# A third exponentials buffer, grouped sample products and six banks for the K/V slabs in the attention stream of a hybrid decoder step

## The chip, the cores and the metric

The kernel runs on one core of one Trainium2 chip. The metric is the device time of one execution in microseconds. Everything is float32; the large products are split into a high and a low part (three products each).

## The reference, cut to what matters

Four half-layers over 1024 prompt tokens and 32 sample tokens (8 sequences of 4). First an mLSTM layer and its MLP, then K and V are projected once, then one sliding-window attention layer with its MLP, then a final norm.

```
kv = rmsnorm(x, kv_norm) @ w_kv                    # shared K/V: 4 heads of 64
q  = rmsnorm(x, norm_mix[l]) @ w_q[j]              # 16 query heads of 64
s  = einsum(q, k) * 64**-0.5 + bias                # prompt: blocks of 128 queries on 256 keys
s  = where(valid, s, -inf)                         # sample: 32 rows on 128 cached + 4 new keys
m  = maximum(max(s), sink)
e  = exp(s - m)
p  = e / (sum(e) + exp(sink - m))
x  = x + (p @ v) @ w_attn_out[j]
x  = x + relu(rmsnorm(x, norm_ffn[l]) @ w_up)**2 @ w_down
```

What is in question is the middle of this: the K/V projection, and the attention with its q and output projections. Outputs are the two hidden states, the mLSTM states and the key and value windows.

## The kernel before

All activations are held transposed, features on partitions and the 1056 tokens along the free dimension, in three blocks of 352 tokens. Each engine has one hand-written instruction stream, in order; they meet at counting semaphores. Weights come in slabs of 128x1024 numbers, two buffers: SP loads a slab, ACT rounds it (`w_hi`, L682), DVE makes the remainder (`w_lo`, L1031), and PE multiplies.

The attention part has 20 slabs in the order `ATT`: kv2 and kv3 (values), kv0 and kv1 (keys), q0 to q5, four output slabs, q6, q7, four output slabs. A slab is eight chunks; a chunk is nine matmuls of 352 columns (L1864 to L1866: three token blocks by three products). Block g of a slab's output has one of four PSUM banks (`att_block`, L345: g % 4), and before PE starts block g it waits until block g-4 has been taken by DVE (L1424 for K/V, L1426 for q, L1443 for output slabs). The blocks of K/V need the token scale `rstd`: its sums are two matmuls inside slab kv2 (L1623, L1624, L1627), after which DVE (L1049) and ACT (L715) finish it.

The values are needed with tokens on partitions. After chunk 18 PE transposes all of them at once (sixteen transposes, L1962) into banks 4 to 7 and DVE copies them to `v_tok` (L1528). The last pieces follow after chunk 34 (L1973, L1540 to L1542). SP waits for the first copies (`kvt_taken`, L610) before it loads the sample's cache into `act_a` and `act_b`, and the loads of later slabs are behind that in its queue.

From chunk 42 on the attention runs as 64 units (8 head pairs by 8 blocks of 128 queries). Unit u's steps are spread over the engines' loops. In iteration u of its loop, each engine does the following:

- PE: `scores(u+1)` into banks 4 and 5, the dense chunks of `att_window(u)` (one chunk in each of iterations 0 to 29, then 0 to 6), `transposes(u-1)` into bank 6, `values(u-2)` into bank 7, and a step of the sample. 
- DVE: `maxima(u)` (L1460: adds the bias and writes the logits to `prob`, with the maxima), `probabilities(u-1)` (L1467, L1470), `outputs(u-3)` (L1476), then the dense evacuations and splits of the window, then a step of the sample.
- ACT: `exps(u)` (L881), dense splits, `copy_t(u-1)` (L890, the transposed probabilities out of PSUM), and at u % 8 == 2 the rounding of a finished head pair (`o_high`, L897).
- POOL: the sink column of unit u (L1005), and at u % 8 == 3 a remainder (`o_low`, L997).

`prob` has two buffers (u % 2). So `maxima(u)` and the sink column of u wait for the transposes of u-2:

```
if u >= 2:
    dve.wait_ge(t_ready, u - 1)
```

PE's `scores(u)` waits for `maxima(u-1)` (`mx_ready`), since banks 4 and 5 are single.

The sample (all 8 sequences, per half of the heads) runs as steps 0 to 8 beside units 23 to 31 and again beside 55 to 63. Step 6 multiplies probabilities and values: in each of two halves, for each of four sequences, a product over 128 cached keys and one over the 32 new ones, both into the same 32 partitions of the bank, one after the other (L1947, L1948). Its probabilities are first copied from the bank to `sp_t` and `sp_new` (L1506, L1507). The scores of steps 2 and 3 (L1932, L1933) have the same order.

Of the kernel before, what the change touches and what calls it, by code (L numbers as in the profile page):

```python
# [20 lines left out]
P = 128  # L21
# [6 lines left out]
TB = 3  # L28
# [154 lines left out]
def build(nc, io):  # L183
    with ExitStack() as ctx:
# [114 lines left out]
        k_past, v_past = (x[:, 0:DEC_B * P].rearrange("p (b n) -> p b n", b=DEC_B) for x in (act_a, act_b))  # L299
        prob = sb("prob", [P, 2, 2, 2 * WIN + 2], where=phase)  # L300
        prob_t = sb("prob_t", [P, 2, 4, P], where=phase)
        stat = sb("stat", [P, 2, 6], where=phase)
        s_stat = sb("s_stat", [P, 6], where=phase)
# [3 lines left out]
        s_prob = sb("s_prob", [P, 2, SKEY + 1], where=phase)  # L307
        sp_t = sb("sp_t", [P, 2, P], where=phase)
        sp_new = sb("sp_new", [SAMP, 2, P], where=phase)
        phase.close()  # L310
# [34 lines left out]
        def att_block(g):  # L345
            return acc[:, g % 4, 0:TN]

# [120 lines left out]
        def _(sp):  # L468
# [138 lines left out]
            def load_cache(gp):  # L607
                heads = slice(2 * gp, 2 * gp + 2)
                if gp == 0:
                    sp.wait_ge(kvt_taken, 1)  # L610
                for dst, name, last_read in ((k_past, "cache_k", 2), (v_past, "cache_v", 6)):
                    if gp > 0:
                        sp.wait_ge(sk_ready, last_read)
                    sp.dma_start(dst, io[name][:, :, heads, :].rearrange("b s g d -> s b (g d)")
                                 ).then_inc(samp_in, 16)

            def store_kv():
                sp.wait_ge(kvt_taken, 2)
# [55 lines left out]
        def _(act):  # L674
# [201 lines left out]
            def exps(u):  # L876
                r, lo = u % 2, WIN if u % NCH == 0 else 0
# [74 lines left out]
        def _(pool):  # L952
# [48 lines left out]
            for u in range(UNITS):  # L1001
                n = u // NCH
                if u >= 2:
                    pool.wait_ge(t_ready, u - 1)
                nc.gpsimd.tensor_copy(prob[:, u % 2, :, 2 * WIN], by_head[:, n // 4, n % 4]).then_inc(sink_col, 1)  # L1005
# [12 lines left out]
        def _(dve):  # L1018
# [431 lines left out]
            def maxima(u):  # L1450

                n, b = divmod(u, NCH)
                r, lo, head = u % 2, WIN if b == 0 else 0, 8 * (n // 4) + n % 4
                if u >= 2:
                    dve.wait_ge(t_ready, u - 1)
                if b == 0:
# [7 lines left out]
            def probabilities(u):  # L1464
                r, lo = u % 2, WIN if u % NCH == 0 else 0
# [12 lines left out]
            def sample(gp, step):  # L1478
# [25 lines left out]
                if step == 6:  # L1504
                    dve.wait_ge(sk_ready, 7 * gp + 5)
                    V.tensor_copy(sp_t[:], bank[:, 0:256].rearrange("p (a n) -> p a n", a=2))  # L1506
                    V.tensor_copy(sp_new[:], bank[0:SAMP, 256:512].rearrange("p (a n) -> p a n", a=2)).then_inc(sk_taken, 1)  # L1507
                if step == 7:
# [15 lines left out]
            dve.wait_ge(rstd_ready, 3)  # L1524
            att_dense(range(4, 22))
            dve.wait_ge(kvt_ready, 1)
            for q in range(4):
                x = V.tensor_copy(v_tok[:, 2 * q:2 * q + 2], acc[:, 4 + q].rearrange("p (t n) -> p t n", t=2))  # L1528
            x.then_inc(kvt_taken, 1)
            dve.wait_ge(bias_in, 16)  # L1530
# [7 lines left out]
            att_dense(range(32, 36))  # L1538
            dve.wait_ge(kvt_ready, 2)
            V.tensor_copy(v_tok[0:SAMP, NCH], acc[0:SAMP, 4, 0:256])  # L1540
            V.tensor_copy(k_new[:, 0], acc[:, 5, 0:256])
            V.tensor_copy(k_new[0:SAMP, 1], acc[0:SAMP, 5, 256:512]).then_inc(kvt_taken, 1)  # L1542
            att_dense(range(36, 42))
# [30 lines left out]
        def _(pe):  # L1574
# [261 lines left out]
            def att_dense(chunks):  # L1836

                for i in chunks:
# [17 lines left out]
                    for b in range(TB):  # L1856
                        g = BLK0 + TB * (AFIRST[p] + n) + b
                        if kk == 0 and g >= BLK0 + 4:
                            pe.wait_ge(blk_taken, g - 3)
                        elif kk == 0:  # L1860
                            pe.wait_ge(out_taken, O_KV - (1 if g < BLK0 + 3 else 0))
                        if (kind, j, k, b) == ("q", 5, 0, 0):
# [11 lines left out]
            def scores(u):  # L1874
                n, b = divmod(u, NCH)
                gp, lo = n // 4, WIN if b == 0 else 0
                if b == 0:
                    pe.wait_ge(q_ready, n + 1)
                if u == 0:
                    pe.wait_ge(kvt_taken, 2)  # L1880
                else:
                    pe.wait_ge(mx_ready, u)
# [6 lines left out]
            def transposes(u):  # L1889
                r = u % 2  # L1890
                pe.wait_ge(pr_ready, u + 1)
                if u >= 1:
                    pe.wait_ge(tc_ready, u)
                for e in range(2):
# [18 lines left out]
            def sample(gp, step):  # L1913
# [12 lines left out]
                if step in (2, 3):  # L1926
# [3 lines left out]
                    for b in range(4):  # L1930
                        rows = slice(SAMP * b, SAMP * b + SAMP)
                        T.matmul(bank[rows, 0:WIN], q_m[:, 4 * half + b], kp_t[:, 4 * half + b], start=True, stop=True)  # L1932
                        x = T.matmul(bank[rows, WIN:SKEY], q_m[:, 4 * half + b], k_t[:, gp, SEQ:], start=True, stop=True)  # L1933
                    x.then_inc(sk_ready, 1)
# [6 lines left out]
                if step == 6:  # L1941
                    pe.wait_ge(sk_taken, 6 * gp + 5)
                    for half in range(2):
                        for b in range(4):
                            rows = slice(SAMP * b, SAMP * b + SAMP)
                            out = bank[rows, P * half:P * half + P]
                            T.matmul(out, sp_t[:, half, rows], v_past[:, 4 * half + b], start=True, stop=False)  # L1947
                            x = T.matmul(out, sp_new[:, half, rows], v_tok[0:SAMP, NCH, P * gp:P * gp + P], start=False, stop=True)  # L1948
# [9 lines left out]
            pe.wait_ge(ssum_taken, 6)  # L1958
            for t in range(NCH):
                for g, v in enumerate((act_a, act_b)):  # L1960
                    at = 256 * (t % 2) + P * g
                    x = T.transpose(acc[:, 4 + t // 2, at:at + P], v[:, cols(t)], ident[:])  # L1962
            x.then_inc(kvt_ready, 1)
            att_dense(range(19, 35))
            pe.wait_ge(blk_taken, BLK0 + 4 * TB)
            pe.wait_ge(kvt_taken, 1)
            for g, v in enumerate((act_a, act_b)):
                T.transpose(acc[0:SAMP, 4, P * g:P * g + P], v[:, cols(NCH)], ident[:])
            for i, t in enumerate((NCH - 1, NCH)):
                n = size(t)  # L1970
                for g in range(2):
                    at = 256 * i + P * g
                    x = T.transpose(acc[0:n, 5, at:at + P], k_t[:, g, cols(t)], ident[:])  # L1973
            x.then_inc(kvt_ready, 1)
# [98 lines left out]
```

## Time and profile before

| | |
|---|---|
| three runs | 2568.69, 2572.0, 2572.22 us, median 2572.0 |
| profiled execution, its own time | 2562.05 us |
| its span | 2560.2 us, mean granted TensorE clock 0.984 |
| PE busy | 2453.5 us (96%) |
| PE weight loads | 2331.1 us (91%) |
| DVE, ACT, POOL busy | 1155.2, 656.1, 159.5 us |
| attention part, first K/V matmul to last output chunk | about 1364 to 1782 us of the span |

The profile lists PE twice: weight loads (PEld) and matmuls (PE). A matmul's end is modelled and overlaps its follower, so a row of PE that reads "busy" may still hold a stop; the idle time printed beside a weight load is the nearer measure of how long PE stood. Numbers in square brackets are the idle time of that engine just before the row, with what ended it.

### The profile page before, as it was taken

The numbers are of one execution on the slowest core, as the hardware profiler recorded it, in microseconds if no ns is written. First come the engines' busy times: TensorE is split into PE (matmuls) and PEld (weight loads), VectorE is DVE, ScalarE is ACT, GpSimd is POOL, SyncE is SP. The second block draws the span as 40 slices with busy tenths as digits, with TensorE's granted clock in tenths as the row PEclk, the third lists the DMA queues.
The fourth block names the chain that finished last, engine by engine and source line by source line (L and its number), as shares of the span: only waits on it lengthen the run. The fifth ranks groups of instructions, "written<-read, shape, count | busy, mean of one in ns | idle before, by whom it ended". The sixth has DMA issues, their size and how long they took to land.

```text
span 2560.2 us, 36896 instructions
## 1 busy us (share of the span) xinstructions
PE 2453.5 (96%) x15530; PEld 2331.1 (91%) x15530; DVE 1155.2 (45%) x2023; ACT 656.1 (26%) x1080; POOL 159.5 (6%) x208
## 2 busy tenths in 40 slices
PE   6999999988999999999998989989999999999998
PEld 6889898877999999999998866868999999999997
DVE  6545555566434333333345554465433333333333
ACT  3232222233212111111222443254212112112113
POOL 3000000002000000000002011013000000000002
PEclk8999999999999999999999998999999999999999
DMA  3111121110111111111111311101111111111111
GB/s 108 44 46 52 46 64 37 43 35 25 50 50 50 42 42 50 42 44 47 44 47 53 91 28 46 34 9 41 42 45 47 42 50 42 42 50 50 42 50 68
DMA packets 177416, 120.53 MB, mean 47 GB/s; under 512 B 23624, under 2 KB 173045, under 8 KB 177221
## 3 DMA queue, kind: packets, MB, share of 16 engines
q1 hardware_dynamic: 177108, 118.10, 15.7%
q8 instruction: 132, 2.16, 0.4%
q14 instruction: 32, 0.25, 0.0%
q10 hardware_dynamic: 144, 0.02, 0.0%
HBM read 110.94 MB, written 12.33 MB: 48 GB/s over the span
## 4 chain that ended last, share of the span: by engine, by line
PE 89%; DVE 7%; issue 1%; ACT 1%; POOL 1%; DMA 1%; SPq 0%; DVEq 0%; ACTq 0%
PE acc L1589 58%; PE acc L1669 5%; PE acc L1671 4%; PE acc L1670 4%; PE acc L1864 3%; PE acc L1866 3%; PE acc L1865 3%; DVE prob L1460 2%; PE acc L1885 2%; DVE rstd L1049 1%; PE acc L1897 1%; PE acc L1725 1%; DVE w_lo L1031 1%; PE acc L1692 1%; PE acc L1710 1%
## 5 line engine op out<-in xcount | busy, mean ns | idle before, releaser
L1589 PE MATMUL acc<-x_hi,w_hi 128*128 128x352 f32 x1560 | 340.0, 326 | 14.8 <-DVE x_lo L1037 6.2
L682 ACT ACTIVATE w_hi<-w_raw 128x1024 fp32r<-128x1024 f32 x180 | 189.2, 1051 | 618.4 <-PE acc L1589 527.6
L1062 DVE TENSOR_TENSOR x_res<-x_res,acc 128x1056 f32<-128x1056 f32 x128 | 160.4, 1253 | 413.6 <-PE acc L1589 413.6
L1589 PE MATMUL acc<-x_hi,w_lo 128*128 128x352 f32 x1560 | 336.6, 323 | 0.0
L1589 PE MATMUL acc<-x_lo,w_hi 128*128 128x352 f32 x1560 | 336.4, 324 | 0.0
L1589 PE MATMUL acc<-h_hi,w_hi 128*128 128x352 f32 x1536 | 332.1, 324 | 0.0
L1589 PE MATMUL acc<-h_hi,w_lo 128*128 128x352 f32 x1536 | 331.1, 323 | 0.0
L1589 PE MATMUL acc<-h_lo,w_hi 128*128 128x352 f32 x1536 | 330.6, 323 | 0.0
L1589 PEld LDWEIGHTS acc<-x_hi,w_hi 128*128 128x128 f32 x1560 | 266.0, 189 | 18.1 <-issue 13.0
L1589 PEld LDWEIGHTS acc<-x_hi,w_lo 128*128 128x128 f32 x1560 | 268.0, 188 | 0.0
L1589 PEld LDWEIGHTS acc<-x_lo,w_hi 128*128 128x128 f32 x1560 | 265.6, 188 | 0.0
L1589 PEld LDWEIGHTS acc<-h_hi,w_lo 128*128 128x128 f32 x1536 | 263.6, 188 | 0.0
L1589 PEld LDWEIGHTS acc<-h_hi,w_hi 128*128 128x128 f32 x1536 | 261.7, 189 | 0.0
L1589 PEld LDWEIGHTS acc<-h_lo,w_hi 128*128 128x128 f32 x1536 | 260.9, 188 | 0.0
L1031 DVE TENSOR_TENSOR w_lo<-w_raw,w_hi 128x1024 fp32r<-128x1024 f32 x180 | 236.8, 1316 | 21.5 <-ACT w_hi L682 21.4
L1055 DVE TENSOR_TENSOR act_a<-acc,rstd 128x1056 f32<-128x1056 f32 x64 | 80.5, 1257 | 331.9 <-PE acc L1589 329.6
L1669 PE MATMUL acc<-x_hi,w_hi 128*128 128x352 f32 x576 | 197.4, 343 | 2.6 <-DVE pair L1177 2.6
L845 ACT ACTIVATE act_b<-act_a 128x1056 f32<-128x1056 f32 x64 | 69.6, 1087 | 501.8 <-DVE act_a L1055 501.8
L1671 PE MATMUL acc<-x_hi,w_lo 128*128 128x352 f32 x576 | 188.4, 327 | 0.0
L1670 PE MATMUL acc<-x_lo,w_hi 128*128 128x352 f32 x576 | 188.0, 326 | 0.0
L1669 PEld LDWEIGHTS acc<-x_hi,w_hi 128*128 128x128 f32 x576 | 110.5, 192 | 11.1 <-issue 4.6
L1385 DVE TENSOR_TENSOR h_lo<-act_a,h_hi 128x1056 fp32r<-128x1056 f32 x64 | 80.6, 1259 | 73.8 <-ACT h_hi L847 73.8
(265 smaller groups left out, 3112.1 us busy)
## 6 DMA issues: line engine op xcount, KB each, us to landing
w_raw<-in_w_up SPq DMA_DIRECT2D x64, 512.0 KB
w_raw<-in_w_down SPq DMA_DIRECT2D x64, 512.0 KB
w_raw<-in_w_mlstm_in SPq DMA_DIRECT2D x24, 512.0 KB
x_in<-in_x_prompt SPq DMA_DIRECT2D x8, 512.0 KB, 4.0
w_raw<-in_w_mlstm_out SPq DMA_DIRECT2D x8, 512.0 KB
w_raw<-in_w_q SPq DMA_DIRECT2D x16, 256.0 KB
w_raw<-in_w_attn_out SPq DMA_DIRECT2D x16, 256.0 KB
out_y_prompt<-y_out SPq DMA_DIRECT2D x8, 512.0 KB, 2.6
```

The costliest lines, as they stand in the source:

```text
L682: nc.scalar.activation(w_hi[:, s.parity], w_raw[:, s.parity], ACT.Copy).then_inc(hi_split, 1)
L1031: V.tensor_tensor(w_lo[:, s.parity], w_raw[:, s.parity], w_hi[:, s.parity].bitcast(F32), ALU.subtract).then_inc(lo_split, 1)
L1055: x = V.tensor_tensor(blocks(dst), group(o), blocks(rstd[:]), ALU.mult)
L1062: V.tensor_tensor(blocks(x_res[:, k]), blocks(x_res[:, k]), group(o), ALU.add).then_inc(out_taken, 1)
L1385: V.tensor_tensor(h_lo[:, half, c], act_a[:], h_hi[:, half, c].bitcast(F32), ALU.subtract).then_inc(hl_ready, 1)
L1589: last = T.matmul(out[:, b], w[:, k, m], x[:, TN * b:TN * b + TN], start=(k == 0 and i == 0), stop=(k == k_chunks - 1 and i == 2))
L1669: T.matmul(block_of(g), hi, mh[:, span(b)], start=(kk == 0), stop=False)
L1670: T.matmul(block_of(g), hi, ml[:, span(b)], start=False, stop=False)
L1671: x = T.matmul(block_of(g), lo, mh[:, span(b)], start=False, stop=(kk == n_k - 1))
L1864: T.matmul(att_block(g), hi, mh[:, span(b)], start=(kk == 0), stop=False)
L1865: T.matmul(att_block(g), hi, ml[:, span(b)], start=False, stop=False)
L1866: x = T.matmul(att_block(g), lo, mh[:, span(b)], start=False, stop=(kk == n_k - 1))
```

## The change

Three edits. `prob` and `stat` get three buffers; `maxima`, the sink column, `exps`, `probabilities` and `transposes` use u % 3, and the waits of DVE and POOL are for the transposes of u-3. To make room, `sp_t` and `sp_new` move into `act_a`, where the cached keys have been read by then; the second load of the keys waits for step 6.

In sample steps 2, 3 and 6 the four products on the cache are issued first, then the four on the new tokens.

The blocks of the four K/V slabs rotate over six banks, (g - BLK0) % 6, and wait for block g-6; later blocks stay with four. Banks 4 and 5 are thus in use, so the value transposes use banks 6 and 7 alone, in two halves: after chunk 18 and after chunk 20. `kvt_taken` counts three steps; the cache load waits for the second, and the wait for the third moves from `scores(0)` to `transposes(0)`.

```
-        prob = sb("prob", [P, 2, 2, 2 * WIN + 2], where=phase)
+        sp_t = act_a[:, 0:2 * P].rearrange("p (a n) -> p a n", a=2)
+        sp_new = act_a[0:SAMP, 2 * P:4 * P].rearrange("p (a n) -> p a n", a=2)
+        prob = sb("prob", [P, 3, 2, 2 * WIN + 2], where=phase)
...
         def att_block(g):
-            return acc[:, g % 4, 0:TN]
+            bank = g % 4 if g >= BLK0 + 4 * TB else (g - BLK0) % 6
+            return acc[:, bank, 0:TN]
...
             def load_cache(gp):
-                    sp.wait_ge(kvt_taken, 1)
-                for dst, name, last_read in ((k_past, "cache_k", 2), (v_past, "cache_v", 6)):
+                    sp.wait_ge(kvt_taken, 2)
+                for dst, name, last_read in ((k_past, "cache_k", 6), (v_past, "cache_v", 6)):
...
-                if u >= 2:
-                    pool.wait_ge(t_ready, u - 1)
+                if u >= 3:
+                    pool.wait_ge(t_ready, u - 2)
...
             def maxima(u):
-                r, lo, head = u % 2, WIN if b == 0 else 0, 8 * (n // 4) + n % 4
-                if u >= 2:
-                    dve.wait_ge(t_ready, u - 1)
+                r, lo, head = u % 3, WIN if b == 0 else 0, 8 * (n // 4) + n % 4
+                if u >= 3:
+                    dve.wait_ge(t_ready, u - 2)
...
-            att_dense(range(4, 22))
-            dve.wait_ge(kvt_ready, 1)
-            for q in range(4):
-                x = V.tensor_copy(v_tok[:, 2 * q:2 * q + 2], acc[:, 4 + q].rearrange(...))
-            x.then_inc(kvt_taken, 1)
+            att_dense(range(4, 20))
+            for i in range(2):
+                dve.wait_ge(kvt_ready, i + 1)
+                for q in range(2):
+                    x = V.tensor_copy(v_tok[:, 4 * i + 2 * q:4 * i + 2 * q + 2], acc[:, 6 + q].rearrange(...))
+                x.then_inc(kvt_taken, 1)
+                att_dense(range(20 + i, 21 + i))
...
                         g = BLK0 + TB * (AFIRST[p] + n) + b
-                        if kk == 0 and g >= BLK0 + 4:
+                        if kk == 0 and g >= BLK0 + 5 * TB:
                             pe.wait_ge(blk_taken, g - 3)
+                        elif kk == 0 and g >= BLK0 + 2 * TB:
+                            pe.wait_ge(blk_taken, g - 5)
...
             def transposes(u):
-                r = u % 2
+                r = u % 3
                 pe.wait_ge(pr_ready, u + 1)
-                if u >= 1:
-                    pe.wait_ge(tc_ready, u)
+                pe.wait_ge(*((kvt_taken, 3) if u == 0 else (tc_ready, u)))
...
                 if step == 6:
                     for half in range(2):
                         for b in range(4):
                             rows = slice(SAMP * b, SAMP * b + SAMP)
+                            T.matmul(bank[rows, P * half:P * half + P], sp_t[:, half, rows], v_past[:, 4 * half + b],
+                                     start=True, stop=False)
+                        for b in range(4):
+                            rows = slice(SAMP * b, SAMP * b + SAMP)
                             out = bank[rows, P * half:P * half + P]
-                            T.matmul(out, sp_t[:, half, rows], v_past[:, 4 * half + b], start=True, stop=False)
                             x = T.matmul(out, sp_new[:, half, rows], v_tok[0:SAMP, NCH, P * gp:P * gp + P], start=False, stop=True)
...
             att_dense(range(19))
-            for t in range(NCH):
-                for g, v in enumerate((act_a, act_b)):
-                    x = T.transpose(acc[:, 4 + t // 2, at:at + P], v[:, cols(t)], ident[:])
-            x.then_inc(kvt_ready, 1)
-            att_dense(range(19, 35))
+            for i in range(2):
+                if i == 1:
+                    pe.wait_ge(kvt_taken, 1)
+                for t in range(4 * i, 4 * i + 4):
+                    for g, v in enumerate((act_a, act_b)):
+                        x = T.transpose(acc[:, 6 + t % 4 // 2, at:at + P], v[:, cols(t)], ident[:])
+                x.then_inc(kvt_ready, 1)
+                att_dense(range(19 + 2 * i, 21 + 2 * i))
+            att_dense(range(23, 35))
```

## Rows read from the trace of the kernel before

**Rows 1.** The page: busy times of the engines, shares of the span, instructions.
```profile
PE 2453.5 (96%) x15530; PEld 2331.1 (91%) x15530; DVE 1155.2 (45%) x2023; ACT 656.1 (26%) x1080; POOL 159.5 (6%) x208
```

**Rows 2.** Timeline (start, length in us) of PE, early in slab kv3.
```profile
1377.54 0.32 PE L1865 MATMUL acc<-x_lo,w_hi 128*128 128x352 f32 x1
1377.70 0.32 PE L1866 MATMUL acc<-x_hi,w_lo 128*128 128x352 f32 x1
1384.78 0.66 PE L1864 MATMUL acc<-x_hi,w_hi 128*128 128x352 f32 x1 [6.75 <-DVE act_a L1424]
```

**Rows 3.** Timeline of DVE and ACT, same slabs.
```profile
1376.29 6.75 DVE L1049 RECIPROCAL rstd<-rstd 128x1056 f32<-128x1056 f32 x1
1384.19 1.38 DVE L1424 TENSOR_TENSOR act_a<-acc,rstd 128x352 f32<-128x352 f32 x3 [1.15 <-ACT rstd L715]
1385.50 1.21 DVE L1031 TENSOR_TENSOR w_lo<-w_raw,w_hi 128x1024 fp32r<-128x1024 f32 x1
1398.13 1.06 ACT L682 ACTIVATE w_hi<-w_raw 128x1024 fp32r<-128x1024 f32 x1 [13.02 <-PE acc L1866]
```

**Rows 4.** Waits from 1437 to 1745 us: us in total, times, longest.
```profile
PEld acc L1885 <- DVE stat L1460: 34.2, 49, 2.1
...
PEld acc L1885 <- issue: 6.4, 13, 1.2
```

**Rows 5.** Timeline of a usual unit, DVE and weight loads.
```profile
1470.42 0.48 DVE L1460 CUSTOM_DVE_ANT_0 prob<-acc,bias,sinks 128x256 f32<-128x256 f32 x1 [1.95 <-PE acc L1897]
1471.37 0.30 PEld L1885 LDWEIGHTS acc<-k_t,q_t 64*128 64x128 f32 x4 [0.64 <-DVE stat L1460]
1471.82 0.28 DVE L1476 COPY q_t<-acc 128x128 f32<-128x128 f32 x1
...
1474.92 0.30 PEld L1885 LDWEIGHTS acc<-k_t,q_t 64*128 64x128 f32 x4 [0.64 <-DVE stat L1460]
```

**Rows 6.** Timeline: score loads behind something other than the transposes.
```profile
1439.05 0.30 PEld L1885 LDWEIGHTS acc<-k_t,q_t 64*128 64x128 f32 x4 [1.08 <-DVE stat L1460]
...
1459.50 0.48 DVE L1460 CUSTOM_DVE_ANT_0 prob<-acc,bias,sinks 128x256 f32<-128x256 f32 x1
1460.45 0.30 PEld L1885 LDWEIGHTS acc<-k_t,q_t 64*128 64x128 f32 x4 [1.16 <-DVE stat L1460]
...
1699.96 0.30 PEld L1885 LDWEIGHTS acc<-k_t,q_t 64*128 64x128 f32 x4 [1.16 <-DVE stat L1460]
```

**Rows 7.** Timeline: a score load whose data was long there.
```profile
1528.12 0.30 PEld L1885 LDWEIGHTS acc<-k_t,q_t 64*128 64x128 f32 x4 [0.17 <-issue]
```

**Rows 8.** Window: us; PE, PEld, DVE, ACT, POOL busy; clock. Waits, 1701 to 1717.3.
```profile
1704.00:1708.00 4.00, 4.00 (x35) 2.49 (x32) 3.68 (x18) 2.75 (x9) 0.19 (x1) 1.00 0.01 2
...
PEld acc L1885 <- DVE stat L1460: 1.3, 4, 0.6
```

**Rows 9.** Weight loads: step 6 of both halves, step 2.
```profile
1551.10 0.14 PEld L1947 LDWEIGHTS acc<-act_b,sp_t 128*32 128x32 f32 x2 [1.00 <-DVE sp_new L1507]
1558.73 0.51 PEld L1885 LDWEIGHTS acc<-k_t,q_t 64*128 64x128 f32 x4 [0.38 <-issue]
...
1718.77 0.14 PEld L1947 LDWEIGHTS acc<-act_b,sp_t 128*32 128x32 f32 x2 [0.17 <-issue]
1724.10 0.30 PEld L1885 LDWEIGHTS acc<-k_t,q_t 64*128 64x128 f32 x4 [0.20 <-issue]
...
1535.08 0.18 PEld L1932 LDWEIGHTS acc<-kp_t,q_m 128*32 128x32 f32 x8 [0.17 <-issue]
1535.55 0.30 PEld L1885 LDWEIGHTS acc<-k_t,q_t 64*128 64x128 f32 x4
```

**Rows 10.** A window as in rows 8, and step 7's loads in both halves.
```profile
1556.00:1560.00 4.00, 4.00 (x15) 1.43 (x16) 0.43 (x1) 0.00 (x0) 0.00 (x0) 0.50 0.00 0
...
1562.00 0.29 PEld L1953 LDWEIGHTS acc<-ident,s_prob 128*128 128x128 f32 x2 [0.33 <-issue]
...
1725.91 0.20 PEld L1953 LDWEIGHTS acc<-ident,s_prob 128*128 128x128 f32 x2 [0.17 <-issue]
```

More of the change, by code:

```diff
@@ L299, in build @@
         k_past, v_past = (x[:, 0:DEC_B * P].rearrange("p (b n) -> p b n", b=DEC_B) for x in (act_a, act_b))
-        prob = sb("prob", [P, 2, 2, 2 * WIN + 2], where=phase)
+        sp_t = act_a[:, 0:2 * P].rearrange("p (a n) -> p a n", a=2)
+        sp_new = act_a[0:SAMP, 2 * P:4 * P].rearrange("p (a n) -> p a n", a=2)
+        prob = sb("prob", [P, 3, 2, 2 * WIN + 2], where=phase)
         prob_t = sb("prob_t", [P, 2, 4, P], where=phase)
-        stat = sb("stat", [P, 2, 6], where=phase)
+        stat = sb("stat", [P, 3, 6], where=phase)
         s_stat = sb("s_stat", [P, 6], where=phase)
@@ L307, in build @@
         s_prob = sb("s_prob", [P, 2, SKEY + 1], where=phase)
-        sp_t = sb("sp_t", [P, 2, P], where=phase)
-        sp_new = sb("sp_new", [SAMP, 2, P], where=phase)
         phase.close()
@@ L617, in store_kv @@
             def store_kv():
-                sp.wait_ge(kvt_taken, 2)
+                sp.wait_ge(kvt_taken, 3)
                 for new, name in ((k_new[:, 0, :], "k_prompt"), (v_tok[:, NCH - 1, :], "v_prompt")):
@@ L876, in exps @@
             def exps(u):
-                r, lo = u % 2, WIN if u % NCH == 0 else 0
+                r, lo = u % 3, WIN if u % NCH == 0 else 0
                 act.wait_ge(mx_ready, u + 1)
@@ L1002, in _ @@
                 n = u // NCH
-                if u >= 2:
-                    pool.wait_ge(t_ready, u - 1)
-                nc.gpsimd.tensor_copy(prob[:, u % 2, :, 2 * WIN], by_head[:, n // 4, n % 4]).then_inc(sink_col, 1)
+                if u >= 3:
+                    pool.wait_ge(t_ready, u - 2)
+                nc.gpsimd.tensor_copy(prob[:, u % 3, :, 2 * WIN], by_head[:, n // 4, n % 4]).then_inc(sink_col, 1)
                 if u >= 11 and u % 8 == 3:
@@ L1464, in probabilities @@
             def probabilities(u):
-                r, lo = u % 2, WIN if u % NCH == 0 else 0
+                r, lo = u % 3, WIN if u % NCH == 0 else 0
                 dve.wait_ge(ex_ready, u + 1)
@@ L1505, in sample @@
                     dve.wait_ge(sk_ready, 7 * gp + 5)
-                    V.tensor_copy(sp_t[:], bank[:, 0:256].rearrange("p (a n) -> p a n", a=2))
-                    V.tensor_copy(sp_new[:], bank[0:SAMP, 256:512].rearrange("p (a n) -> p a n", a=2)).then_inc(sk_taken, 1)
+                    V.tensor_copy(sp_t, bank[:, 0:256].rearrange("p (a n) -> p a n", a=2))
+                    V.tensor_copy(sp_new, bank[0:SAMP, 256:512].rearrange("p (a n) -> p a n", a=2)).then_inc(sk_taken, 1)
                 if step == 7:
@@ L1524, in _ @@
             dve.wait_ge(rstd_ready, 3)
-            att_dense(range(4, 22))
-            dve.wait_ge(kvt_ready, 1)
-            for q in range(4):
-                x = V.tensor_copy(v_tok[:, 2 * q:2 * q + 2], acc[:, 4 + q].rearrange("p (t n) -> p t n", t=2))
-            x.then_inc(kvt_taken, 1)
+            att_dense(range(4, 20))
+            for i in range(2):
+                dve.wait_ge(kvt_ready, i + 1)
+                for q in range(2):
+                    x = V.tensor_copy(v_tok[:, 4 * i + 2 * q:4 * i + 2 * q + 2], acc[:, 6 + q].rearrange("p (t n) -> p t n", t=2))
+                x.then_inc(kvt_taken, 1)
+                att_dense(range(20 + i, 21 + i))
             dve.wait_ge(bias_in, 16)
@@ L1538, in _ @@
             att_dense(range(32, 36))
[L1539 to L1542, printed above, removed]
+            dve.wait_ge(kvt_ready, 3)
+            V.tensor_copy(v_tok[0:SAMP, NCH], acc[0:SAMP, 6, 0:256])
+            V.tensor_copy(k_new[:, 0], acc[:, 7, 0:256])
+            V.tensor_copy(k_new[0:SAMP, 1], acc[0:SAMP, 7, 256:512]).then_inc(kvt_taken, 1)
             att_dense(range(36, 42))
@@ L1857, in att_dense @@
                         g = BLK0 + TB * (AFIRST[p] + n) + b
-                        if kk == 0 and g >= BLK0 + 4:
+                        if kk == 0 and g >= BLK0 + 5 * TB:
                             pe.wait_ge(blk_taken, g - 3)
+                        elif kk == 0 and g >= BLK0 + 2 * TB:
+                            pe.wait_ge(blk_taken, g - 5)
                         elif kk == 0:
-                            pe.wait_ge(out_taken, O_KV - (1 if g < BLK0 + 3 else 0))
+                            pe.wait_ge(out_taken, O_KV - (1 if g < BLK0 + TB else 0))
                         if (kind, j, k, b) == ("q", 5, 0, 0):
@@ L1878, in scores @@
                     pe.wait_ge(q_ready, n + 1)
-                if u == 0:
-                    pe.wait_ge(kvt_taken, 2)
-                else:
+                if u > 0:
                     pe.wait_ge(mx_ready, u)
@@ L1945, in sample @@
                             rows = slice(SAMP * b, SAMP * b + SAMP)
+                            T.matmul(bank[rows, P * half:P * half + P], sp_t[:, half, rows], v_past[:, 4 * half + b],
+                                     start=True, stop=False)
+                        for b in range(4):
+                            rows = slice(SAMP * b, SAMP * b + SAMP)
                             out = bank[rows, P * half:P * half + P]
-                            T.matmul(out, sp_t[:, half, rows], v_past[:, 4 * half + b], start=True, stop=False)
                             x = T.matmul(out, sp_new[:, half, rows], v_tok[0:SAMP, NCH, P * gp:P * gp + P], start=False, stop=True)
@@ L1958, in _ @@
             pe.wait_ge(ssum_taken, 6)
-            for t in range(NCH):
-                for g, v in enumerate((act_a, act_b)):
-                    at = 256 * (t % 2) + P * g
-                    x = T.transpose(acc[:, 4 + t // 2, at:at + P], v[:, cols(t)], ident[:])
-            x.then_inc(kvt_ready, 1)
-            att_dense(range(19, 35))
+            for i in range(2):
[3 more added lines that the diff above has]
+                    for g, v in enumerate((act_a, act_b)):
+                        at = 256 * (t % 2) + P * g
+                        x = T.transpose(acc[:, 6 + t % 4 // 2, at:at + P], v[:, cols(t)], ident[:])
+                x.then_inc(kvt_ready, 1)
+                att_dense(range(19 + 2 * i, 21 + 2 * i))
+            att_dense(range(23, 35))
             pe.wait_ge(blk_taken, BLK0 + 4 * TB)
-            pe.wait_ge(kvt_taken, 1)
+            pe.wait_ge(kvt_taken, 2)
             for g, v in enumerate((act_a, act_b)):
-                T.transpose(acc[0:SAMP, 4, P * g:P * g + P], v[:, cols(NCH)], ident[:])
+                T.transpose(acc[0:SAMP, 6, P * g:P * g + P], v[:, cols(NCH)], ident[:])
             for i, t in enumerate((NCH - 1, NCH)):
@@ L1972, in _ @@
                     at = 256 * i + P * g
-                    x = T.transpose(acc[0:n, 5, at:at + P], k_t[:, g, cols(t)], ident[:])
+                    x = T.transpose(acc[0:n, 7, at:at + P], k_t[:, g, cols(t)], ident[:])
             x.then_inc(kvt_ready, 1)
```

## The prediction

> **What bounds the kernel now.** I read the page's busy times first: PE is busy 96% of the span, every other engine under half [rows 1]. So time is gained only where PE stands, or where its clock is low. The windows over the attention part (1364 to 1782 us) show both, at three places, and the change has an edit for each. The timelines and the table of waits then say what ends each stop.
>
> The first is at the start of slab kv3: PE has done three of its 72 matmuls and stands 6.75 us until DVE's first evacuation [rows 2], which waits for the reciprocal of 6.75 us and the root behind it [rows 3]. The first matmul afterwards lasts 0.66 us where its kind took 0.32 just before [rows 2]: the clock had fallen.
>
> The second is once in nearly every unit. The reader is to follow one round: `maxima` starts at 1470.42, released by the transposes, and `scores` starts 0.95 us later, released by `maxima`, having stood 0.64 us; the next round is 3.55 us on and the same [rows 5]. The waits sum to 34.2 us in 49 times [rows 4].
>
> The third is the sample's step 6: 16 pairs of loads from 1551.10 to 1558.73 in the first half of the heads, 1718.77 to 1724.10 in the second [rows 9], with the clock at 0.50 in the first [rows 10].
>
> **K/V slabs on six banks.** kv3's three blocks no longer wait for kv2's evacuation. From 1377.70 the remaining 69 matmuls go on at the pitch of 0.16 us [rows 2]: 1377.70 + 69 x 0.16 = 1388.7 for the last start; with 0.32 for it and 0.05 for the signal ACT's rounding of the next slab starts at 1389.1, where it started at 1398.13 [rows 3]. That is 9.0 us: 6.75 of stop, the rest the clock. What must be there at 1388.7: the remainder of slab kv0, done at 1385.50 + 1.21 = 1386.7, and kv2's first block taken, by about 1384.7 [rows 3]. So the 2.0 us of slack cover both; if the root came 3 us later, 1 us would come back. The value transposes stay sixteen; that they are in two halves adds a PE wait for two copies, covered by the two chunks between, and DVE work in the same amount. The cache load sits on SP's queue until the second copies, about three us of PE's work later than now, with the q slabs' loads queued behind it; their slabs are needed some twenty chunks on. I take these at nothing. Without a covering row I bound them by 2 us lost. Ends for the edit: 6.7 and 9.0; taken 9.0.
>
> **Third buffer.** `maxima(u)` then waits for the transposes of u-3, done a round earlier, and for `scores(u)`, which PE issues at the head of the round before. In a round of 3.55 us [rows 5] it can be done some 1.7 us in, and PE asks for it at the end. What does not vanish: a score load whose data was long there stands 0.17 us too [rows 7].
>
> The sum over all score loads: 34.2 us in 49 waits, and of the 6.4 us in 13 under "issue" six (4.7 us) are the same stop by position, seven are the 0.2 to 0.4 us ones [rows 4]. So 38.9 us in 55. From this comes off:
> - Ten that end with another thing. The first is the stream's start, 1.08 us; where DVE evacuates a q slab before the next `maxima`, as at 1460.45, `maxima` starts at 1459.50 without waiting for PE [rows 6], and the third buffer can't bring it earlier. Four such of 1.16 us (the last at 1699.96), further 1.22, 1.27, 0.86, 0.37, and 2.06 us behind the sample's step 8. Together 11.5 us.
> - Five from 1701 to 1717 (1.3 us in four [rows 8], and one of 0.7): there are no dense chunks there, and DVE is busy 3.68 of 4 us [rows 8], so DVE is the bound. 2.0 us, taken as kept.
>
> 38.9 - 11.5 - 2.0 = 25.4 us in 40 waits, of which 40 x 0.17 = 6.8 stay: 18.6 us gained. What is late next in the usual round: nothing on PE; DVE's `outputs(u-3)` will be what DVE waits for, with the values one round old. The ends: 0, if another wait takes the place; 38.9 - 55 x 0.17 = 29.6, if every one goes. I take 18.6.
>
> **Grouped products.** At full clock step 6 takes 5.33 us for 16 pairs, 0.333 a pair, of which most is a pause at each change between 128-row and 32-row products [rows 9]. Step 2 has sixteen loads of 32 columns without such a change in 0.47 us [rows 9], so eight take 0.24. The new order has four groups of eight with one pause each. By the rows a group is 0.24 + 0.2 = 0.44; I take 0.5, as eight products of 128 columns have less to overlap with than step 2's mix. 5.33 - 4 x 0.5 = 3.3 us a half, 6.7 in both. Ends: 0, if the pause comes with every product, and 7.1. Steps 2 and 3 have no pause to lose: nothing.
>
> The pause is the trace's (rows 9: 0.333 us a pair against 0.06 for a pair of step 2). The Trainium skill ("TensorEngine Tiling (Array Packing)", Key Properties) says that changing the tiling mode, not just the tile, drains the engine; by that rule the order by shape is what counts, and the trace agrees. Against the change speaks another sentence of it ("TensorE: Matmul & The Clock Gate", Part 3, The mechanism): loads overlap running matmuls only when the row group differs, and here all four products of a group use the same rows. By that rule a group would be 8 x (27 + 53) ns + 0.2 = 0.84 us, an estimate from the page's column times, and the edit would give 2.0 us a half instead of 3.3: 2.7 us less in all. Step 2 has the same row group throughout and its 0.47 us speak for the shorter time.
>
> **Clock.** The first half's step 6 took 7.63 us against 5.33 in the second: 2.3 us at the low clock [rows 9]. From the load of `scores` behind it to step 7's it took 1562.00 - 1558.73 = 3.27 us, in the second half 1725.91 - 1724.10 = 1.81 [rows 9, 10]: 1.5 us. The clock fell while PE worked at a third of its density; with 2 us of products in place of 5.3 I expect no fall there: 3.8 us. The second half had the same sparse 5.3 us with no fall, so this is a matter of phase, and may not repeat: ends 0 and 5, and a fall elsewhere could cost 3.
>
> **Sum.** 9.0 + 18.6 + 6.7 + 3.8 = 38.1 us. The profiled execution's own time is 2562.05 us (span 2560.2): 2524 us. The three runs had 2568.69, 2572.0 and 2572.22, 10 us above it at the median; I carry the difference over: 2572.0 - 38.1 = 2534 us.
>
> **Rivals.** (a) The units find another stop. For it: DVE's stream is in order, with `outputs`, the splits of 1.21 us and evacuations of 1.4 us between two `maxima`, and ACT has its exponentials behind `copy_t`, which waits for PE. Against it: each is needed a round later than it is issued. If two thirds of the 18.6 are lost: 2534 + 12 = 2546 us. (b) The products keep their pauses, by each change of column group, and the clock falls as before: 2534 + 6.7 + 3.8 = 2544 or 2545 us. Against it the 0.47 us of step 2. (c) The other side: the deeper rotation makes DVE wait in every unit for the values before it gets to `maxima`. Now `outputs` never waits in the stretch shown (it starts right after the probabilities [rows 5]); then DVE is a round ahead and it will. Were this for the values of the same round, `maxima` would begin after them and the 0.28 us copy. PE's value loads end 0.64 us before 1471.37, at 1470.73; with 0.3 for the last product, 0.28 for the copy and 0.95 for `maxima`, `scores` starts at 1472.2 or 0.85 us later than before [rows 5]. In 62 units 53 us, against 19.5 from the other edits: 2572 + 33 = 2605 us. It decides if the awaited values lie less than 1.7 us before `maxima`'s due time; the code takes those of u-3, a whole round older. (d) The six banks only move the stop: kv0 waits for its weights or the copies hold up PE, and 7 us of the 9 come back: 2541 us.
>
> **Chances.** Forecast 0.72, (a) 0.14, (b) 0.06, (c) 0.04, (d) 0.04. About 0.2% (5 us) is what a measurement of this kernel can tell from no change. Faster than that holds in all but (c) and in combinations of (a), (b) and (d): 0.92; within it 0.03, slower 0.05. Range: the high end of the terms, with some of the ten or five waits gone too, gives 2523; (a) together with part of (b) gives 2556.
>
> **What would show it.** In the profile after: no idle time before L1864 near 1378, and ACT's rounding of the next slab at about 1389; `maxima` no longer released by the transposes but by L1885, and before most score loads 0.17 instead of 0.64 us; 1.16 us kept before the score load after each q slab's last chunk; waits of L1885 for L1460 down from 34 to about 12 us; step 6 in 2 us; no window at 0.50 after it. Wrong would be: `transposes` (L1897) waiting for L1470 in units with a dense chunk, or DVE's copy of the outputs ahead of each `maxima` with PE standing behind it; loads of step 6 still 0.17 us apart; kv0 late for `w_lo`.

## The result, and the profile after

The changed kernel takes 2527.45 us at the median of four runs (2526.38 to 2529.18), beside 2570.35 us for the kernel before (2564.59 to 2572.22, four runs). The ratio is 0.9841, 95% interval 0.982 to 0.9862: 1.6% faster. The forecast was 2534 us.

To see where it went I take one stretch out of both profiles: from the first sum matmul of the K/V norm to the same matmul of the last MLP. In the chain that ended last (start, length) they are, before:

```profile
1371.31 0.86 PE acc L1623 x2
...
1789.63 0.86 PE acc L1623 x2
```

and after:

```profile
1375.63 0.86 PE acc L1626 x2
...
1754.89 0.86 PE acc L1626 x2
```

418.3 us became 379.3: 39.1 us less. (It is one profile for each kernel; two more of the changed kernel, below, have 379.4 and 377.8 us.) Before this stretch the profiled run after is 4.3 us later than the one before (stages that were not changed), behind it 1.9 us longer; so the two profiled executions, 2562.05 and 2529.18 us, differ by only 32.9 us. The profiled run before was a quick one. I judge the terms by the stretch and not by the two totals.

The start of kv3. ACT's rounding of the slab behind it (timeline of ACT):

```profile
1393.34 1.06 ACT L683 ACTIVATE w_hi<-w_raw 128x1024 fp32r<-128x1024 f32 x1 [3.91 <-PE acc L1871]
```

That is 17.71 us behind the sum matmul; it was 1398.13 - 1371.31 = 26.82 us [rows 3]. PE no longer stands for DVE anywhere in kv3: from 1378 us to the first score load, at 1432.98, no weight load has idle time before it. The clock stays at 1.00 in all windows of this part.

The usual unit, and one with a q slab's last chunk (timelines of DVE and weight loads; the pair to rows 5 and 6):

```profile
1446.34 0.48 DVE L1461 CUSTOM_DVE_ANT_0 prob<-acc,bias,sinks 128x256 f32<-128x256 f32 x1 [0.44 <-PE acc L1888]
1448.78 0.30 PEld L1888 LDWEIGHTS acc<-k_t,q_t 64*128 64x128 f32 x4 [0.17 <-issue]
1448.91 0.29 DVE L1477 COPY q_t<-acc 128x128 f32<-128x128 f32 x1 [0.94 <-PE acc L1911]
...
1452.12 0.48 DVE L1461 CUSTOM_DVE_ANT_0 prob<-acc,bias,sinks 128x256 f32<-128x256 f32 x1
1453.07 0.30 PEld L1888 LDWEIGHTS acc<-k_t,q_t 64*128 64x128 f32 x4 [1.16 <-DVE stat L1461]
```

`maxima` is now released by the scores themselves, 1.5 us before PE asks for them, and the score load stands 0.17 us. DVE's new wait, for the values, is there too (0.94 us) and costs nothing. The last two lines are the case that a buffer can't help: the same 1.16 us as in rows 6. The table of waits over the units (total, times, longest) says it for all:

```profile
PEld acc L1888 <- DVE stat L1461: 11.6, 12, 2.1
DVE prob L1461 <- PE acc L1888: 11.5, 22, 2.5
PEld acc L1888 <- issue: 9.4, 48, 1.2
PEld acc L1899 <- DVE prob L1471: 4.3, 8, 1.6
```

34.2 us in 49 [rows 4] became 11.6 in 12.

Step 6 of the sample (weight loads), first half of the heads:

```profile
1535.92 0.16 PEld L1950 LDWEIGHTS acc<-act_b,act_a 128*32 128x32 f32 x8 [1.25 <-DVE act_a L1508]
1536.27 0.15 PEld L1955 LDWEIGHTS acc<-v_tok,act_a 32*32 32x32 f32 x8 [0.20 <-issue]
1536.62 0.16 PEld L1950 LDWEIGHTS acc<-act_b,act_a 128*32 128x32 f32 x8 [0.20 <-issue]
1536.98 0.15 PEld L1955 LDWEIGHTS acc<-v_tok,act_a 32*32 32x32 f32 x8 [0.20 <-issue]
1537.33 0.30 PEld L1888 LDWEIGHTS acc<-k_t,q_t 64*128 64x128 f32 x4 [0.20 <-issue]
```

1.41 us, where it was 7.63 in the first and 5.33 in the second half [rows 9]. Each product of the code is two loads here.

Laid end to end, the stretch is shorter by 9.0 us up to the first score load, 10.5 from there to step 6, 6.2 in it, 1.5 to step 7's load, 8.9 to the second step 6 and 3.9 in that, and longer by 1.0 behind it: 39.1 us. The 1.0 us is the clock, which fell here after step 8 and did not before (windows as in rows 8; the clock is the 0.74 and the 0.83):

```profile
1692.00:1696.00 4.00, 2.64 (x13) 2.42 (x10) 1.65 (x6) 1.71 (x4) 0.00 (x0) 0.74 0.00 0
1696.00:1700.00 4.00, 4.00 (x31) 3.10 (x29) 0.29 (x1) 1.33 (x2) 1.49 (x1) 0.83 0.00 0
```

### The profile page after: what moved, and what is told of

It is laid out like the page before. It is cut to its first block, busy times and chain, and to the rows that moved or that the text cites. A ratio compares the mean times of both kernels' runs of the same rounds, so it can differ in the third digit from the quotient of the medians.

```text
span 2527.4 us, 36895 instructions
## 1 busy us (share of the span) xinstructions
PE 2442.5 (97%) x15530; PEld 2330.6 (92%) x15530; DVE 1164.1 (46%) x2023; ACT 651.7 (26%) x1080; POOL 160.1 (6%) x208
## 3 DMA queue, kind: packets, MB, share of 16 engines
q8 instruction: 133, 2.18, 0.4%
## 4 chain that ended last, share of the span: by engine, by line
PE 90%; DVE 5%; ACT 1%; issue 1%; DMA 1%; POOL 1%; SPq 0%; DVEq 0%; ACTq 0%
PE acc L1592 59%; PE acc L1672 5%; PE acc L1674 4%; PE acc L1673 4%; PE acc L1869 3%; PE acc L1871 3%; PE acc L1870 3%; PE acc L1888 1%; PE acc L1911 1%; PE acc L1899 1%; PE acc L1728 1%; DVE w_lo L1032 1%; PE acc L1695 1%; DVE rstd L1050 1%; PE acc L1713 1%
## 5 line engine op out<-in xcount | busy, mean ns | idle before, releaser
L1384 DVE TENSOR_TENSOR act_a<-act_a,act_b 128x1056 f32<-128x1056 f32 x64 | 80.5, 1258 | 73.8 <-ACT act_b L846 73.8
```

The lines of the kernel that those rows point to most:

```text
L1384: V.tensor_tensor(act_a[:], act_a[:], act_b[:], ALU.mult).then_inc(act_ready, 1)
```

## The experiments

The length below is that of the same stretch in the profiled run; the kernel before has 418.3 us, the changed one 379.3. Ratios are to the kernel before.

**Each edit alone.** First the six banks, with the split value transposes:

```
+            bank = g % 4 if g >= BLK0 + 4 * TB else (g - BLK0) % 6
+            return acc[:, bank, 0:TN]
```

> The kernel before with the six K/V banks and the split value transposes alone; prob keeps two buffers and the sample products their old order. Theory (each edit removes its own stop and they add up): the stop of 6.75 us before slab kv3's fourth matmul and the low clock behind it go, ACT's rounding of the slab after it comes 9.0 to 9.3 us sooner relative to the sum matmuls, nothing else moves: 9 us less than the kernel before, ratio about 0.9965. Rival (the time comes back as later waits, the head start of PE being lost by the first units): less than 3 us at the first score product. Rival (the edits need each other): over 12 us or under 6 us.

2553.27 us, ratio 0.9959 (0.9944 to 0.9974); stretch 406.9 us, 11.5 less. Up to the first score load it is 57.34 us, where it was 66.37: the edit's own 9.0, and it does not come back. The rest is luck of the clock. The order of step 6 is the old one here, and it took 5.33 us in both halves: the first half's clock stayed up until step 7 was through and fell only then (0.82 and 0.75 from 1552 to 1560 us), which saved 2.3 + 1.5 us; behind the second half it fell too (0.80 and 0.77 from 1716 to 1724 us), and the part behind step 6 is 1.5 us longer. The two ends of the first half's step 6 in the timeline of weight loads:

```profile
1543.27 0.14 PEld L1949 LDWEIGHTS acc<-act_b,sp_t 128*32 128x32 f32 x2 [1.00 <-DVE sp_new L1508]
...
1548.60 0.30 PEld L1888 LDWEIGHTS acc<-k_t,q_t 64*128 64x128 f32 x4 [0.20 <-issue]
```

Then the third buffer:

```
-        prob = sb("prob", [P, 2, 2, 2 * WIN + 2], where=phase)
+        prob = sb("prob", [P, 3, 2, 2 * WIN + 2], where=phase)
```

> The kernel before with the third buffer of prob and stat (and sp_t, sp_new in act_a) alone. Theory: score loads stand 0.17 instead of 0.64 us in some 40 units, the ten that something else holds stay, the waits of the score loads for the maxima fall from 34 to about 12 us: 18 to 19 us less, ratio about 0.993. The clock of the first step 6 may stay low for 10 us as before (then no gain there) or not (then up to 4 us more). Rival (the deeper rotation gains only with the shorter step 6): under 12 us.

2547.21 us, ratio 0.9937 (0.9917 to 0.9957); stretch 399.5 us, 18.8 less. All idle times before the 64 score loads add up to 21.0 us, where they were 40.7. Step 6 took 7.54 us in the first half: the clock was low as in the kernel before.

Then the order of the products, as in the diff of the change:

> The kernel before with the order of the sample products alone. Theory (a pause of 0.20 us per change of the rows, 4 changes instead of 16 in each half of the heads): step 6 takes 1.4 us instead of 7.6 and 5.3 us, and the window behind the first has the full clock: 3.9 + 6.2 + 1.5 = 11.6 us less, ratio about 0.9955. If the low clock there belongs to the unit stops as well and not only to step 6, it stays low somewhere in the first units after step 6 and 1 to 4 us of this are missing.

2554.23 us, ratio 0.9965 (0.9951 to 0.9979); stretch 407.0 us, 11.3 less. Step 6 took 1.42 us in both halves. The expected 11.6 held; the clock was 0.59 from 1561 to 1565 us, some 7 us behind step 6, much as in the changed kernel.

> The changed kernel on this chip, as the sum against which the three parts are held. If the parts are independent, its gain is that of the three together, 39 us in the attention part (9 + 18.7 + 11.6), 38 to 44 us in all. If two of them share a stop, it is less than the sum by over 3 us.

2526.7 us, ratio 0.9848 (0.9822 to 0.9874); stretch 379.4 us. The parts add up to 11.5 + 18.8 + 11.3 = 41.6 us against 39.0 for all. The low clock in the first step 6 and up to step 7's load, 2.3 + 1.5 = 3.8 us, is a gain of the first kernel and of the third, so it is counted twice; from step 7 to the second step 6, and at the start of the stretch, the parts together are 0.8 and 0.5 us short of the whole. The medians of the totals say the same: 11.5 + 17.6 + 10.6 = 39.7 us against 38.1. To within a microsecond or two the edits are independent.

**What the remaining waits are.** DVE takes the next unit's maxima before its dense work and sample step, in every iteration:

```
-                if u < UNITS:
-                    maxima(u)
+                if u == 0:
+                    maxima(0)
                 if 1 <= u <= UNITS:
                     probabilities(u - 1)
                 if u >= 3:
                     outputs(u - 3)
+                if u + 1 < UNITS:
+                    maxima(u + 1)
```

> The changed kernel with one edit: DVE does maxima(u+1) before the dense evacuations, splits and sample step of iteration u, not after them. Theory (what is left of the score loads' waits is DVE's own order, not the buffer): the ten waits kept (1.16 us four times, 1.22, 2.02, 2.06, 0.86, 0.36) fall to about 0.17 us, all but the 1.08 us at the start: 9 us less than the changed kernel, about 2518 us. It works only with the third buffer, as maxima(u+1) needs a buffer free one round early. Rival (PE has to wait for the evacuations themselves, which are now 0.9 us later): the waits move to the dense blocks or to the scores of a new head pair and less than 3 us are gained.

2517.05 us, ratio 0.9823 (0.9799 to 0.9846); stretch 373.8 us, 5.5 less than the changed kernel and not 9. The ten waits are gone, all but that at the start (the idle times before the score loads fall from 21.0 to 11.4 us). Of these 9.6 us, 4.1 came back by the changed kernel's first profile, and 5.6 by its third, which has 377.8 us. They are in the sample's steps (the load of L1936 stands 2.7 us in all, where its like stood 0.7) and in the output slabs' blocks, whose copies DVE now takes 0.9 us later: the wait of their first load for `x_res` (L1869 in the changed kernel, L1871 here) went from 3.6 us in three to 5.0 in five. So part of the rival was true.

**Only where it pays.** The same in seven iterations alone:

```
+AHEAD = (5, 13, 21, 31, 35, 46, 53)
...
-                if u < UNITS:
+                if u < UNITS and u - 1 not in AHEAD:
                     maxima(u)
...
+                if u in AHEAD:
+                    maxima(u + 1)
```

> The changed kernel; DVE takes the next unit's maxima ahead of its other work in seven iterations alone: the six that evacuate a q slab (5, 13, 21, 35, 46, 53; not 29, where a sample step follows) and 31 with the sample's step 8. The kernel with all maxima ahead took 9.3 us off the score loads and gave 3.8 back at the sample's steps and the output slabs' blocks. Theory (the gain is at the seven, the loss at the others): the seven waits of 1.16, 1.16, 1.15, 2.02, 1.22, 1.16 and 2.06 us fall to 0.17, 8.7 us, of which about 1 us comes back where PE waits for step 8's remainder and the transposes: 7 to 8 us less than the changed kernel in the attention part, 2 us less than with all maxima ahead. Rival (what came back belongs to the q slabs' blocks, taken 0.9 us later): no better than all ahead, 5.5 us or less.

2516.13 us, ratio 0.9819 (0.98 to 0.9838). The stretch ends in the chain at

```profile
1375.53 0.86 PE acc L1629 x2
...
1744.75 0.86 PE acc L1629 x2
```

369.2 us, 10.0 less than the changed kernel's first profile; the idle times before the score loads are 12.4 us. Its units cost what the wait says: the load that stood 1.16 us [rows 6] is

```profile
1451.98 0.30 PEld L1891 LDWEIGHTS acc<-k_t,q_t 64*128 64x128 f32 x4 [0.17 <-issue]
```

With it on the same chip:

> All maxima ahead, on the same chip as the selective kernel, for the comparison of the two. Expected 5.5 us less than the changed kernel in the attention part and 2 us more than the selective one.

2520.04 us, ratio 0.9828 (0.9808 to 0.9848), stretch 373.8 us again.

> The changed kernel on the same chip as the two kernels with maxima ahead: 38 to 44 us less than the kernel before, 5 to 8 us more than these two.

2525.45 us, ratio 0.9863 (0.9841 to 0.9884), stretch 377.8 us; here the clock did not fall behind the second half, as it did in the first profile. So the seven are worth 8.6 us against this run and 4.6 more than all 63, where 7 to 8 and 2 were expected. The 8.6 are a balance: the score loads stand 8.7 us less, the fall of the clock behind the first step 8 is missing too, worth about 1.6 us (see the clock, below), and other waits took the rest back. The order alone is thus worth 7 to 8.6 us. In the totals the selective kernel is below the changed one (the intervals of the ratios just part), while between the two kernels with maxima ahead the intervals overlap; their order rests on the stretches. By its stretch it is the fastest kernel of this study.

**The slower rival made real.** DVE's copy of the outputs moved to wait for the values of PE's same round:

```
-                if u >= 3:
-                    outputs(u - 3)
                 att_dense(att_window(u))
+                if 2 <= u < UNITS + 2:
+                    outputs(u - 2)
```

> The changed kernel with the copy of unit u-2's outputs in DVE's iteration u (at its end), so that it waits for the values of PE's same round; otherwise as the changed kernel. This is the slower rival of the prediction made real. By it: DVE starts maxima 0.28 us after the values, scores start about 0.85 us later than in the kernel before and 1.3 us later than in the changed one, in 55 to 62 units: 65 to 80 us more than the changed kernel, about 2600 us. If less than 20 us, then the order of the outputs hardly mattered and the rival's price was wrong.

2607.91 us in one run; stretch 459.0 us, 79.8 more than the changed kernel. The timeline (DVE and weight loads) is the mechanism as the prediction described it: the copy waits for the values, `maxima` begins behind it, and the score load stands until that is done. The lines above the dots are of one unit, those below of the next:

```profile
1455.89 0.29 DVE L1477 COPY q_t<-acc 128x128 f32<-128x128 f32 x1
1456.22 0.48 DVE L1461 CUSTOM_DVE_ANT_0 prob<-acc,bias,sinks 128x256 f32<-128x256 f32 x1
1457.17 0.30 PEld L1888 LDWEIGHTS acc<-k_t,q_t 64*128 64x128 f32 x4 [1.58 <-DVE stat L1461]
...
1460.60 0.29 DVE L1477 COPY q_t<-acc 128x128 f32<-128x128 f32 x1 [2.75 <-PE acc L1911]
1460.80 0.47 DVE L1461 CUSTOM_DVE_ANT_0 prob<-acc,bias,sinks 128x256 f32<-128x256 f32 x1
1461.81 0.33 PEld L1888 LDWEIGHTS acc<-k_t,q_t 64*128 64x128 f32 x4 [1.51 <-issue]
```

Most score loads stand 1.45 us instead of 0.17. All of them together stand 76.3 us, 55.3 more than in the changed kernel; the other 24 us lie mainly in the waits of the transposes for the probabilities (10.1 us, where they were 4.3), in the sample's steps, and in a clock at 0.50 for 12 to 16 us behind each step 6.

**The price of the sample's products.** First the groups cut to two sequences: two products on the cache, two on the new tokens, and so on.

```
-                        for b in range(4):
+                        for b in (0, 1):
...
+                            if b == 2:
+                                for b2 in (2, 3):
```

> The changed kernel with step 6's products in groups of two (two on the cache, two on the new tokens, and so on): 8 changes of the rows in each half of the heads instead of 4. Theory (a fixed pause per change, loads at some 19 ns each): step 6 takes 8 x 0.20 + 32 x 0.019 = 2.2 to 2.3 us instead of 1.41 us. Rival (what counts is that four column groups work side by side): the two-wide group also loses width and takes over 2.6 us.

2.72 us: the theory's 2.3 failed, and the rival's bound of 2.6 holds. The weight loads:

```profile
1535.52 0.14 PEld L1950 LDWEIGHTS acc<-act_b,act_a 128*32 128x32 f32 x4 [1.25 <-DVE act_a L1508]
1535.87 0.14 PEld L1960 LDWEIGHTS acc<-v_tok,act_a 32*32 32x32 f32 x4 [0.20 <-issue]
1536.20 0.14 PEld L1956 LDWEIGHTS acc<-act_b,act_a 128*32 128x32 f32 x4 [0.20 <-issue]
```

Eight groups of four loads take 0.34 us each. With the old order sixteen groups of two take 0.333 each [rows 9], with the new one four groups of eight take 0.353. So a group costs about a third of a microsecond whatever its width up to eight loads, and the law of a pause plus 19 ns a load was wrong: it fits the group of eight only.

Then the products on the cache done four times over:

```
-                        for b in range(4):
+                        for i in range(16):
+                            b = i % 4
```

> The changed kernel with the four products on the cache done four times over in step 6 (the same result, no change of rows between them), 24 more loads and products in each of the four groups. It prices the products themselves. Theory (four column groups side by side, each product 128 columns): the group grows by 24 x 19 to 27 ns = 0.45 to 0.65 us. Rival (products with all 128 rows run one after the other, 128 columns each): 24 x 56 ns = 1.3 us more per group.

```profile
1533.40 0.81 PEld L1951 LDWEIGHTS acc<-act_b,act_a 128*32 128x32 f32 x32 [1.25 <-DVE act_a L1508]
1534.41 0.15 PEld L1956 LDWEIGHTS acc<-v_tok,act_a 32*32 32x32 f32 x8 [0.20 <-issue]
```

2.72 us in all, 1.31 more for 48 more loads with their products: 27 ns each. (The products are repeated in two of the four groups, not in all four as the expectation has it; per group that is 0.65 us, the theory's upper end.) One after the other they would take about 58 ns, an estimate from the pitch of 0.16 us for 352 columns [rows 2] (the expectation's rival says 56). So products of different column groups do overlap, at least two at a time; that all four do is not shown. The first eight loads hide in the price of the change.

## Why the prediction was right, point by point

**The K/V slabs: right.** Forecast 9.0 us, measured 9.0 to the first score load, alone (57.34 us) as with the rest (57.35 us). The slack of 2 us for kv0's weights held. The cover that I took for the cache load and the halved transposes held too: no weight load has idle time before it up to the first score load. That the low clock belongs to this stop is borne out as well: between 1380 and 1392 us it is at 0.50 to 0.53 in the lowest window of each of the three profiles with four banks, and at 1.00 throughout in every one with six.

**The third buffer: right, by slightly wrong items.** Forecast 18.6 us, measured 18.8 alone and 19.4 in the changed kernel (10.5 + 8.9). The ten waits named as staying stayed. By the idle times alone, which the clock hardly touches, the edit is worth 40.7 - 21.0 = 19.7 us. Two items partly cancelled: five waits of the stretch without dense chunks went to 0 to 0.22 us, though DVE was the bound there by its busy time (1.2 us more gained), and the wait of 1.27 us grew to 2.02. There DVE's q evacuation starts 0.03 us after POOL's remainder ends, in both profiles (1586.40 and 1562.08 us), and the score load follows 2.80 us after that end in both; PE asks for it 1.53 us after the end before and 0.78 after. So PE came sooner than the engine it then waits for by way of DVE.

**The products: right in kind, mis-sized.** Forecast 6.7 us at full clock, measured 2 x (5.33 - 1.41) = 7.8, above the upper end of 7.1. The term that failed is the 0.5 us a group: it is 0.35. The rule of the Trainium skill ("TensorEngine Tiling (Array Packing)", Key Properties) that a change of tiling mode drains the engine agrees with all three group sizes. The prediction's estimate of 0.84 us a group from the Trainium skill ("TensorE: Matmul & The Clock Gate", Part 3, The mechanism) does not: a group took 0.353 us, and with the same rows in all four, further loads with their products came every 27 ns.

**The clock: right where it was forecast, wrong in reason.** Forecast 3.8 us, measured 2.3 + 1.5 in and behind the first step 6. But the shorter step 6 is not shown to be the reason. The kernel with the banks alone has the long step 6 at full clock; the changed kernel has a low clock at two other places (0.61 from 1544 to 1548 us, and 0.74 above), which cost part of it back: 1.0 us behind the second step 6, and about 1.6 before it (the kernel with the products four times over, whose clock did not fall there, took 146.3 us from step 7 to the second step 6, and the third profile of the changed kernel 147.9). The prediction's own reserve, that the fall is a matter of phase and may come elsewhere, is what the runs show. In the changed kernel the first of the two falls follows a stop of 2.06 us before the score load behind step 8 (PE busy 2.18 of 4 us), and so it is with the banks alone and with the order alone; the second comes with a stop of 1.57 us before a dense load (PE busy 2.64 of 4 us, in the window shown above):

```profile
1540.00:1544.00 4.00, 2.18 (x18) 1.44 (x18) 2.24 (x12) 2.27 (x10) 0.19 (x1) 0.97 0.27 66
1544.00:1548.00 4.00, 4.00 (x17) 4.00 (x17) 1.32 (x7) 0.81 (x1) 0.00 (x0) 0.61 0.01 4
```

In the three profiles with maxima taken ahead, where the stop of 2.06 us is gone, the clock does not fall there; but in one profile that has the stop (the products four times over) it does not fall either. What decides stays open.

**The sum.** 38.1 us were forecast; the stretch gave 39.1, and between the medians of the four runs each it was 42.9. The remaining 4 us are outside the stretch and the size of the runs' own spread; on two other chips the medians are 38.1 us apart both times. Adding 10 us for the distance between the profiled run and the median was too much: with more runs the medians of the kernel before lay at 2570.35, 2564.79, 2562.28 and 2563.52 us, three of them within 3 us of the profiled 2562.05, and those of the changed kernel at 2525 to 2527 us. So the forecast of 2534 was high mainly by starting from 2572.0. That the sum of the terms came within 1 us is in part luck: the products gave 1.1 us more than forecast and the buffer 0.8, and the clock took 1.0 back.

**The rivals.** (a), another stop in the units, did not come. (b), pauses by column group, is excluded by 27 ns a product. (c) is real when it is built in, but that 2605 us were forecast and 2607.9 measured is partly luck: the forecast was 33 us above the kernel before, the run is 45.6 above that kernel's median on its chip (40.7 in the stretch). The score loads stand 76.3 us where they stood 40.7, 36 us more and not 53; the rest came from other waits and the clock. In the changed kernel it stays away because the code awaits values a whole round old: DVE waits for them 34 times, while the score loads' idle times fall to 21.0 us. (d) did not come.

## What to carry to other kernels

Sort the waits of one kind by what ends each before pricing a deeper rotation: here 40 of 55 were the buffer's and went. Ten were not: one is the start of the stream, and nine are the order of work on the releasing engine, which no buffer helps. All nine fell when maxima were taken ahead everywhere, for 4 to 5.5 us net, because work that was passed over is itself awaited elsewhere; the seven largest alone were worth 7 to 8.6 us. And on PE, put all products of one shape together; for small products like these it is the number of changes that is paid.

## What was not expected of the hardware

A group of products of one shape between changes from 128-row to 32-row form cost 0.333, 0.34 and 0.353 us for two, four and eight loads, and each load with its 128-column product beyond these 27 ns. With the old order of step 6, the clock fell to its lower level (0.50, 1.2 of 2.4 GHz) during the first step 6 in two profiles (the kernel before and the third buffer alone) and stayed at 1.00 through it in a third (the banks alone), where it fell some 3 us behind it; the units before it were alike (113.42 us from the first score load to step 6 in the kernel before, 113.36 with the banks alone).
